# A layer's fill-in matmul chains, halved around the turns of the attention units

## The reference

```python
proj = x @ w_in[l]     # q, k, v of two attentions, latents of a third, gates of three branches
na_out  = neighbourhood_attention(na_q, na_k, na_v, rpb)       # 8 heads of 64
df_out  = diff_attention(df_q, df_k, df_v, lambda, subln_g)    # 4 heads, two softmaxes each
mla_out = latent_attention(c_q, c_kv, k_rope, w_qb, w_kvb)     # 8 heads, low-rank q and kv
merged  = sum(sigmoid(gate_b) * (out_b @ w_branch[b]) for b in 0, 1, 2)
x = layer_norm(ALPHA * x + merged @ w_out)
x = layer_norm(ALPHA * x + (silu(x @ w_g) * (x @ w_u)) @ w_ffn_out)
```

## Time and profile before

| | us |
|---|---|
| median of 3 runs (3850.6 to 3855.64) | 3853.87 |
| the profiled execution's own time | 3858.09 |
| its span, first to last instruction | 3856.3 |
| TensorE matmuls busy in the span | 3486.8 |
| VectorE, ScalarE, GpSimd busy | 1267.3, 952.6, 266.7 |

### The profile page before, as it was taken

How to read it: one execution, slowest core, us unless ns; L and a number is a source line. 1 busy time by engine, 2 the same in 40 slices (tenths; PEclk the granted TensorE clock), 3 DMA queues, 4 the chain that set the end, 5 groups by cost and what they waited for, 6 DMA issues and landing times.

```text
span 3856.3 us, 40245 instructions
## 1 busy us (share of the span) xinstructions
PE 3486.8 (90%) x15232; PEld 2376.6 (62%) x15232; DVE 1267.3 (33%) x1878; ACT 952.6 (25%) x1552; POOL 266.7 (7%) x233
## 2 busy tenths in 40 slices
PE   6888899799959999859989998999799999989996
PEld 6546746744444434247747776887577567768874
DVE  1225610110130011245443345333355443453334
ACT  1111111000020000124454323221244443322212
POOL 0004400200010000002111100000011111000000
PEclk6898898599969999979999999999899999999998
DMA  4101023221149999631202222223321112213221
GB/s 150 66 1 66 23 87 118 101 87 66 43 180 409 409 409 409 256 98 56 68 12 72 66 93 77 88 92 89 74 74 48 35 56 70 95 66 97 89 83 60
DMA packets 266672, 436.99 MB, mean 113 GB/s; under 512 B 10224, under 2 KB 180592, under 8 KB 265712
## 3 DMA queue, kind: packets, MB, share of 16 engines
q1 hardware_dynamic: 266336, 432.48, 31.9%
q0 software_dynamic: 144, 1.90, 0.1%
HBM read 432.25 MB, written 2.10 MB: 113 GB/s over the span
## 4 chain that ended last, share of the span: by engine, by line
PE 49%; DVE 3%; ACT 1%; DVEq 1%; issue 1%; ACTq 0%; DMA 0%; POOLq 0%
PE bank L1823 42%; PE bank L1866 2%; PE bank L1883 1%; PE bank L1902 1%; PE bank L1439 1%; PE bank L1872 1%; PE bank L1897 1%; ACT ring_r L2000 1%; DVE ring_r L2120 0%; DVE x_r L1480 0%; DVEq L2165 0%; DVE layers_norm_rstd L1466 0%; DVE layers_work L2234 0%; DMA layers_con<-in_con 0%; DVEq L2214 0%
## 5 line engine op out<-in xcount | busy, mean ns | idle before, releaser
L1823 PE MATMUL bank<-experts_x_hi_r,ring_r 128*128 128x512 f32 x1800 | 610.8, 404 | 72.8 <-DVE ring_r L2120 57.8
L1823 PE MATMUL bank<-x_r,ring_r 128*128 128x512 f32 x1440 | 575.2, 399 | 0.0
L2120 DVE TENSOR_TENSOR ring_r<-ring,ring_r 128x2048 fp32r<-128x2048 f32 (+2 forms) x162 | 324.3, 2002 | 448.5 <-ACT ring_r L2000 435.9
L1823 PEld LDWEIGHTS bank<-experts_x_hi_r,ring_r 128*128 128x128 f32 x1800 | 343.7, 191 | 186.5 <-issue 92.9
L1823 PE MATMUL bank<-ring_r 128*128 128x512 f32 (+1 forms) x1272 | 403.7, 378 | 0.7 <-DVE x_r L1480 0.7
L1823 PE MATMUL bank<-layers_work_r,ring_r 128*128 128x512 f32 x1312 | 392.9, 401 | 10.0 <-DVE layers_work_r L2258 10.0
L2000 ACT ACTIVATE ring_r<-ring 128x2048 fp32r<-128x2048 f32 (+2 forms) x162 | 272.7, 1683 | 496.0 <-PE bank L1823 472.3
L233 PE MATMUL bank<-xm,ring 128*128 128x512 f32 (+1 forms) x832 | 321.1, 546 | 0.0
L1823 PEld LDWEIGHTS bank<-x_r,ring_r 128*128 128x128 f32 x1440 | 273.6, 190 | 65.0 <-issue 1.0
L1823 PEld LDWEIGHTS bank<-layers_work_r,ring_r 128*128 128x128 f32 x1312 | 249.7, 190 | 79.5 <-issue 18.8
L1823 PEld LDWEIGHTS bank<-ring_r 128*128 128x128 f32 x1272 | 232.6, 188 | 50.6 <-DVE x_r L1480 1.6
(11 more groups left out here) (312 smaller groups left out, 4053.3 us busy)
## 6 DMA issues: line engine op xcount, KB each, us to landing
ring<-in_w_in SPq DMA_DIRECT2D x54, 1024.0 KB, 5.3
ring<-in_w_ffn_in SPq DMA_DIRECT2D x44, 1024.0 KB, 5.1
ring<-in_w_gate SPq DMA_DIRECT2D x30, 1024.0 KB, 18.5
ring<-in_w_in SPq DMA_DIRECT2D x14, 2048.0 KB, 7.8
ring<-in_w_down SPq DMA_DIRECT2D x28, 1024.0 KB, 18.5
ring<-in_w_up SPq DMA_DIRECT2D x26, 1024.0 KB, 18.1
ring<-in_ada_w SPq DMA_DIRECT2D x12, 2048.0 KB, 7.9
mixer_kept<-in_w_down SPq DMA_DIRECT2D x24, 1024.0 KB, 18.5
```

The source lines that it names most:

```text
L1823: last = pe.matmul(out, lhs, rhs, start=start and k == 0, stop=stop and k == len(pairs) - 1)
L2120: dve.tensor_tensor(r32(tile), tile, r32(hi), ALU.subtract).then_inc(done, 1)
```

## The change

In each step the fill-in chains are collected first. The first half of them (rounded up) stays between scores and turn, the others go between turn and values. Nothing else changes: the same events, counts and data.

```diff
     for x in range(last):
         if x < len(units):
             plan.append(("scores", *units[x]))
+        chains = []
         for a, b, fill in fills:
             if a <= x < b:
-                plan += fill[len(fill) * (x - a) // (b - a):len(fill) * (x - a + 1) // (b - a)]
+                chains += fill[len(fill) * (x - a) // (b - a):len(fill) * (x - a + 1) // (b - a)]
+        plan += chains[:(len(chains) + 1) // 2]
         if UNIT_LAG <= x < len(units) + UNIT_LAG:
             plan.append(("turn", *units[x - UNIT_LAG]))
+        plan += chains[(len(chains) + 1) // 2:]
         if x > UNIT_LAG:
             u = units[x - UNIT_LAG - 1]
             plan.append(("values", *u))
```

## The result

Seven runs of each kernel: 3866.19 us after (3864.46 to 3868.59) against 3853.87 before (3850.16 to 3856.0), ratio 1.0034 [1.0023, 1.0046]. The change makes the kernel slower, by 12.3 us where 11 was forecast. The profiled execution took 3868.59 us (span 3866.8), 10.5 more than that of before; its mean granted clock is the same, 0.928.

A forecast was written before the change was run, and what follows sets the result against it. TensorE was taken as the bound, so only its 22 us of standstill and the clock could move. A layer: 6.7 + 1.7 - 1.74 - 1.2 = 5.5 us; two, 11, on 3853.87: 3865 us, range 3855 to 3871.

The forecast's parts named there:

- last turn, wait: Step 49: the turn, without gate.1.6 as cover, waits for inversion and scaling; 4.7 us a layer, lower end 3.9.
- last turn, clock: Step 49: TensorE's clock falls after the turn's wait; 2.0 us a layer, between 0 and 3.
- The bare case: Step 49 if nothing else moved: turn ends at 3279.2 instead of 3275.34 without a wait; 3.9 us of wait.
- ScalarE's copy in step 48: Step 48: ScalarE copies the turn out before rounding the slab, raising step 49's wait from 3.9 to 4.7 us.
- Small losses: Steps 27 (0.45 us), 31 (0.44) and 18 with 16 (0.8, from 0.2): 1.7 us a layer, from 0.6 to 2.1.
- Steps 13 and 14: The 2.2 us bank wait goes, but the next scores still wait for VectorE's copy of step 12's values: 0 us.
- The give-back: Steps 40 and 47: turns inside the slab's-rest waits give 1.74 us a layer, the clock 1.2, from 0 to 2.4.
- The other waits stay: Waits outside the named steps, such as 3.6 us before step 21's turn, do not change: 0 us.
- signs of being wrong: No wait of the last turn, or shorter waits at steps 13, 14 and 21.
- Not slower by the clock: Rival: steps 40 and 47 keep full clock, 4.1 us a layer, step 49 costs 3.9; 3855 to 3859 us; chance 0.16.
- Faster by banks: Rival: earlier turns free banks of steps 13, 14 and 21, some 10 us a layer; 3845 us; chance 0.08.
- ScalarE's queue: Rival: rounding behind turn copies in steps 37, 41, 42, 43, 48, 49 delays chains; 5.4 us more a layer, 3876; chance 0.07.

The follow-up runs named there:

- the first experiment: The changed kernel with the new order in steps 0 to 47 only, steps 48 and 49 as before: 3850.96 us against 3853.6, ratio 0.9996.
- the tail alone: The changed kernel with the new order in steps 48 and 49 only: 3869.64 us against 3853.6 before, ratio 1.0038.
- the earlier inversion: The changed kernel, with VectorE inverting the last unit at gate.1.5 of step 48: 3853.07 us against 3853.6 before, ratio 1.0000.
- step 49 alone: The changed kernel with the new order in step 49 only: 3869.88 us against 3855.08 before, ratio 1.0040.
- the small losses alone: The changed kernel with the new order in steps 16, 18, 27 and 31 only: 3856.78 us against 3855.08 before, ratio 1.0007.

## Why the prediction was right

Its terms for one layer, with what the traces show. What step 47 gave back is taken from the first experiment, whose tail is that of before (2.46 and 2.48 us). "Clock elsewhere" is what steps 21, 22, 27 and 37 differ by beyond their waits.

| us a layer | predicted | layer 1 | layer 2 |
|---|---|---|---|
| last turn, wait | 4.7 | 4.25 | 4.25 |
| last turn, clock | 2.0 | 2.37 | 1.94 |
| steps 18, 27, 31 | 1.7 | 1.81 | 1.84 |
| steps 13, 14 | 0 | +0.88 | +0.07 |
| steps 40 and 47, turn and clock | -2.94 | -4.81 | -3.27 |
| step 21, wait | 0 | -0.31 | -0.33 |
| clock elsewhere | 0 | +1.29 | -2.10 |
| sum (of the steps' starts: 5.49 and 2.46) | 5.5 | 5.48 | 2.40 |

The two layers make 7.95 us. The 2.5 that remain to 10.5 lie outside the changed steps, about half of them from the quick stretch in the trace of before, and the last 1.8 to 12.3 from which execution was traced: that of before took 4.2 us more than its median, that of after 2.4 more. The interval of the medians' difference, 8.9 to 17.7, holds the 11 and lies above the 8. So the mechanism was right, and it was partly luck that the number came within 1.3 us: the traced steps lost 8 us where 11 was forecast, layer 2 less than half of its share.

- **The last turn.** The mechanism is right, and shown from both sides by the tail alone and by the earlier inversion. The bare case ("if nothing else moved") was put at a turn that ends at 3279.2. With step 49 alone, its shift of 6.13 taken off, it ends at 3284.91+0.65-6.13 = 3279.43. But the wait was put at 3.9 and is 3.49 there, and 4.25 with step 48 instead of 4.7. I took the turn's end minus its end without a wait, with some 0.6 us of waiting between its halves; that wait is 0.27, since the first four transposes take 0.65 us and not the 0.45 that I had given them. The clock's share, put at 2.0, came out as 1.8 to 2.4. Against the earlier inversion, which has the same order without the wait, the turn lost 0.3 to 0.6 us and the gate chain 1.0 to 1.6, over the three kernels with the wait.
- **ScalarE's copy in step 48.** Put at 0.8 us (4.7 less 3.9); it is 0.76 of the wait and 0.62 of the stretch.
- **Small losses.** Step 27: 0.45 predicted, 8.34-7.87 = 0.47. Step 31: 0.44 and 0.44. Step 18: 0.8 and 0.90 to 0.94. Its lower end of 0.2 was misread: the row of the swap ends at 2937.86+1.12 = 2938.98 and not by 2938.8, no earlier than the `combine`, so that no row gave the 0.2. The wait there is 0.72.
- **Steps 13 and 14.** The bank wait shrank from 2.17 to 0.33, and in layer 2 the next scores' wait grew from 0.56 to 2.50, 2.7 us together before and 2.8 now. The prediction's "what is late next is the same queue" holds. Missed: step 13 takes 0.27 more in both layers. And in layer 1 the turn of step 14 and the chain behind it now meet three small waits of 0.35, 0.40 and 0.18, for GpSimd and twice for ScalarE.
- **The give-back: the mis-sized term.** The turns inside the waits gave 0.79 and 0.92 us where 0.87 was predicted. For the clock I took half of 2.4, "between the two"; in all four places it was the full one, 1.5 where the chain of before had been slow and 0 where it had been quick. The Trainium skill says that the activity window runs free ("TensorE: Matmul & The Clock Gate", What's actually happening). If position alone decided, the term would have been 0. The traces fit position for waits of one length, of which 15 of 20 were followed by a slow chain (below). But none of 20 was behind the shorter waits, so their length counts too, or the turn that then stands in front of them; no run here separates these two.
- **Step 21 and the clock elsewhere.** "The other waits stay" was wrong for step 21: its wait fell from 3.65 to 3.3 us, and a shorter wait there was one of the prediction's own signs of being wrong. It is 3.3 in each of the four kernels that change steps 16 and 18, and 3.65 in the six that don't, so it comes with what those two steps change. What the clock does behind it and in steps 27 and 37 was not predicted, and these traces do not show what decides it. Of equal waits of 3.3 us before the turn of step 21, after lost the clock in layer 1 and kept it in layer 2. Stretches of after behind each, columns as in the earlier trace rows:

```profile
1885.00:1887.00 2.00, 2.00 (x10) 2.00 (x11) 1.56 (x5) 0.68 (x2) 0.28 (x1) 0.50 0.04 8
1887.00:1889.00 2.00, 2.00 (x8) 0.90 (x6) 0.75 (x1) 1.65 (x6) 0.76 (x1) 0.50 0.00 0
2971.50:2973.50 2.00, 2.00 (x15) 1.28 (x13) 1.31 (x5) 0.93 (x3) 0.53 (x1) 1.00 0.04 8
2973.50:2975.50 2.00, 2.00 (x17) 1.84 (x16) 1.46 (x3) 1.54 (x5) 0.51 (x1) 1.00 0.00 0
```

**The rivals.** Not slower by the clock: half of it came true, since the gate chains of steps 40 and 47 did keep the full clock. It fell with its other half, the clock behind the 4.0 us, which cost some 2 us each time. Faster by banks: the bank wait of step 13 did go, but in layer 2 1.94 us came back as the next wait, as the prediction argued against it; of step 21's wait 0.3 us went, not all of it. ScalarE's queue in steps 37, 41, 42 and 43: no new wait; the starts of steps 38 to 40, and those of 41 to 46, differ from before by the same amount within 0.02 us in both layers. The 1.65 that layer 1 lost in step 37 is scores that took 1.94 and 1.98 us for two groups that take 1.13 and 1.05 before, behind a wait of 0.38 us that both kernels have.

## What to carry to other kernels

When two parts of a static order change places, the price is not in the parts but in what each covered: follow the last item of a pipeline separately, since its preparation has no next item to be hidden under and hangs on whatever was planned in front of it. Look at the queue of the engine that prepares as well as at the order of the engine that waits, for there one short instruction, moved earlier, may take the loss away. And count a chain behind a stall of TensorE at both clocks: in three of four places, shortening a stall by 0.8 us brought back 1.5 us more than itself.

## What the runs showed of the hardware

**A shorter wait kept the clock every time.** The gate chain behind a slab's-rest wait stands at four places of each trace, always 24 matmuls behind two branch chains; where the wait is short, the turn stands between them and the wait. It is measured here from its first row to the first of the next group, in TensorE's order of time (the chain of waits shows 0.1 to 0.2 more). Behind waits of 1.04 to 1.18 us it took 5.78 to 5.79 us in 20 of 20 places (after, and four experiments); behind waits of 1.95 to 1.97 us it took 7.22 to 7.26 in 15 of 20 places and 5.69 to 5.70 in the other five (before, and four experiments).

**Equal waits, different outcomes.** The 3.3 us before step 21's turn, with the same instructions around it, was followed by transposes of 1.11 to 1.12 us in layer 1 and 0.65 to 0.66 in layer 2 (after, the earlier inversion and the small losses alone), and the other way round in the first experiment (0.65, then 1.12). So it kept the clock in four of eight places. Behind the 3.65 us of the six other kernels it was kept in none of twelve: from the turn to the next scores took 2.44 to 2.75 us each time, against 1.48 where the clock was kept. Such a place is worth up to 2.7 us in steps 21 and 22, and a profile of one execution does not say on which side the next one falls.

**The clock can fall behind a wait or in it.** After the 3.98 us before the last turn of layer 2 it was still 1.00 for the first transposes and went to 0.50 within the next 2 us; in layer 1 of the same trace, where the wait of 3.98 us ends at 2199.52, it was 0.97 from 2197 and 0.50 from 2198, before the wait was over.
